# A 272-token encoder layer: the opening laid out by channel, with the squares summed on TensorE and the sine arguments folded on GpSimd

## What is computed

```
h = concatenate([meta, x])                       # 272 x 2048
n = h * rsqrt(mean(h * h, axis=-1) + 1e-6) * norm_g
columns = n @ w_in                               # 2048 x 16384, cut into blocks
z = [t, cos(f w), -sin(f w)]                     # 272 x 33
s = sin(freq * (z @ w1 + b1))
s = sin(freq * (s @ w2 + b2))
s = sin(freq * (s @ w3 + b3))                    # 272 x 64
filters = (s @ w4) * exp(-t * |decay|)
y_a = hyena(u, x1, x2, filters) * silu(gate)     # branch A: long convolution
y_b = fourier(fn_in) * silu(gate)                # branch B: 2-D Fourier transform
y_c = neighbourhood_attention(q, k, v) * silu(gate)
m = g_a * (y_a @ w_a) + g_b * (y_b @ w_b) + g_c * (y_c @ w_c)
out = rmsnorm(h + m @ w_out, final_g)[16:]
```

## Time and profile before

| | us |
|---|---|
| median of 3 runs | 1128.18 |
| lowest, highest | 1127.41, 1128.9 |
| profiled execution | 1127.34 |
| its span in the trace | 1125.5 |
| TensorE busy in the span | 1103.2 |
| VectorE, ScalarE, GpSimd busy | 772.3, 567.1, 61.9 |

### The profile page before, as it was taken

The page is one execution under the profiler, slowest core; times in us unless marked ns, Lnnn a source line. Parts: engine busy times, 40 slices in busy tenths (PEclk is TensorE's granted clock), DMA queues, the critical chain, the costliest instruction groups (busy, mean ns, idle before and its releaser), DMA issues.

```text
span 1125.5 us, 17228 instructions
## 1 busy us (share of the span) xinstructions
PE 1103.2 (98%) x7158; PEld 1005.7 (89%) x7158; DVE 772.3 (69%) x1151; ACT 567.1 (50%) x787; POOL 61.9 (5%) x98
## 2 busy tenths in 40 slices
PE   4999999999999999999999999999999999999997
PEld 2999999999999999999999988888888888888885
DVE  6778888778787688886888785554555455454654
ACT  6655555556545456555554564443444444444443
POOL 4030000300001200002000000000000000000000
PEclk9999999999999999999999999999999999999999
DMA  8744443644335534435543475555555555556652
GB/s 315 241 135 169 150 151 122 205 169 150 135 128 197 186 116 147 151 125 185 188 150 117 160 269 195 202 188 198 187 187 187 192 197 189 201 194 255 231 189 110
DMA packets 30494, 201.54 MB, mean 179 GB/s; under 512 B 3873, under 2 KB 4193, under 8 KB 7745
## 3 DMA queue, kind: packets, MB, share of 16 engines
q1 hardware_dynamic: 25024, 180.16, 45.4%
q0 software_dynamic: 5248, 19.77, 5.3%
q10 hardware_dynamic: 144, 0.52, 0.1%
HBM read 195.19 MB, written 5.24 MB: 178 GB/s over the span
## 4 chain that ended last, share of the span: by engine, by line
PE 98%; DVE 1%; ACT 0%; DMA 0%; issue 0%; DVEq 0%; ACTq 0%
PE ps L574 30%; PE ps L575 30%; PE ps L576 30%; PE ps L579 2%; PE ps L598 1%; PE ps L687 1%; PE ps L727 1%; PE ps L617 1%; PE ps L618 0%; PE ps L718 0%; PE ps L719 0%; PE ps L930 0%; PE ps L729 0%; DMA net<-net_in 0%; PE ps L735 0%; PE ps L737 0%
## 5 line engine op out<-in xcount | busy, mean ns | idle before, releaser
L1328 DVE TENSOR_TENSOR w_lo<-raw,w_hi 128x1024 fp32r<-128x1024 f32 x336 | 409.0, 1230 | 257.8 <-ACT w_hi L988 257.3
L988 ACT ACTIVATE w_hi<-raw 128x1024 fp32r<-128x1024 f32 x336 | 351.2, 1056 | 342.3 <-PE ps L576 340.1
L574 PE MATMUL ps<-xn_hi,w_hi 128*128 128x272 f32 (+2 forms) x1280 | 367.5, 287 | 0.0
L575 PE MATMUL ps<-xn_lo,w_hi 128*128 128x272 f32 (+2 forms) x1280 | 365.7, 286 | 0.0
L576 PE MATMUL ps<-xn_hi,w_lo 128*128 128x272 f32 (+2 forms) x1280 | 365.5, 286 | 0.0
L574 PEld LDWEIGHTS ps<-xn_hi,w_hi 128*128 128x128 f32 x1280 | 242.2, 189 | 2.0
L575 PEld LDWEIGHTS ps<-xn_lo,w_hi 128*128 128x128 f32 x1280 | 241.8, 189 | 0.7
L576 PEld LDWEIGHTS ps<-xn_hi,w_lo 128*128 128x128 f32 x1280 | 242.1, 189 | 0.0
L574 PE MATMUL ps<-w_hi,xg_hi 128*128 128x512 f32 x352 | 137.4, 390 | 0.0
L576 PE MATMUL ps<-w_hi,xg_lo 128*128 128x512 f32 x352 | 137.2, 390 | 0.0
L575 PE MATMUL ps<-w_lo,xg_hi 128*128 128x512 f32 x352 | 137.1, 390 | 0.0
(11 more groups left out here) (265 smaller groups left out, 1394.6 us busy)
## 6 DMA issues: line engine op xcount, KB each, us to landing
raw<-w_stream SPq DMA_DIRECT2D x168, 1024.0 KB, 4.9
branch_y<-ystage POOLq DMA_DIRECT2D x12, 256.0 KB, 3.9
y_raw<-branch_y POOLq DMA_DIRECT2D x3, 1024.0 KB, 7.0
xin<-x SPq DMA_DIRECT2D x2, 1024.0 KB, 6.4
w4s<-w POOLq DMA_DIRECT2D x16, 128.0 KB, 6.0
absd<-decay POOLq DMA_DIRECT2D x8, 256.0 KB, 6.2
h<-x POOLq DMA_DIRECT2D x2, 1024.0 KB, 8.2
rows_t<-rpb POOLq DMA_DIRECT2D x8, 219.0 KB, 6.2
```

The source lines that it names most:

```text
L574: mm(out_ap, a_hi, b_hi, start=first, stop=False)
L575: mm(out_ap, a_hi, b_lo, start=False, stop=False)
L988: A(w_hi[:, w % 2, part, :], raw[:, w % 4, 1024 * part:1024 * part + 1024], ACT.Copy).then_inc(hi_done, 1)
L1328: return V.tensor_tensor(dst, src, hi.bitcast(F32), ALU.subtract)
```

## The change

- **Layout.** The host gives the tokens, meta tokens included, turned: `x_t` has 128 partitions of channels, and on each 16 blocks of 272 tokens. Four transfers (`PIECES`: 5, 5, 4 and 2 blocks) bring them to `x_in`. The 48 transposes go. SyncE starts the first four weight slabs right behind the pieces, without waiting.
- **Sum of squares.** ScalarE squares a piece (`square`), VectorE adds its blocks (`squares_added`, a TENSOR_REDUCE over the block axis, three pieces; the last piece's two blocks are not added), and TensorE adds over the 128 partitions by five float32 products with a matrix of ones, which leaves each token's sum on every partition. ScalarE takes one square root and VectorE one reciprocal of 128x272.
- **Rows.** For each channel block VectorE multiplies by `norm_g` and the reciprocal (`normal`), ScalarE copies the high part (`normal_high`), and VectorE subtracts (`normal_low`). `first_slabs` runs slabs 0 and 1 block by block, both halves for each block.
- **Small network.** ScalarE multiplies the sum by `freq` and adds `freq * b` (`mlp_input`), GpSimd folds in eight dependent steps (`mlp_layer`), of which the second and third layer stand between the issues of its tables. ScalarE takes the sine.
- **Order of the first slabs.** `make_h4`, the filter steps and the weight halves of slabs 2 to 5 are written out in a new order, and the first half of slab 4 runs ahead of `filter_xy(0)`.

```diff
@@ SyncE @@
-            sp.dma_start(xin[0:NM, 2, :], meta).then_inc(x_landed[2], 16)
-            sp.dma_start(xin[:, 0, :], x[0:128, :]).then_inc(x_landed[0], 16)
-            sp.dma_start(xin[:, 1, :], x[128:256, :]).then_inc(x_landed[1], 16)
-            sp.dma_start(ident[:, :], ident_in).then_inc(ident_landed, 16)
-            sp.wait_ge(x_landed[1], 16)
+            for j, (k0, n) in enumerate(PIECES):
+                sp.dma_start(x_in[:, k0:k0 + n, :].rearrange("p k t -> p (k t)"),
+                             x_t[:, L * k0:L * (k0 + n)]).then_inc(x_landed[j], 16)
             for w in range(4):
                 sp.dma_start(raw[:, w, :], w_stream[w]).then_inc(w_landed[w], 16)
+            sp.dma_start(ident[:, :], ident_in).then_inc(ident_landed, 16)
@@ GpSimd @@
+            def pool_linked(ins, n):
+                ins.then_inc(pool_link, 1)
+                pool.wait_ge(pool_link, n)
+
+            def mlp_layer(layer):
+                G = nc.gpsimd
+                n = 7 * layer
+                pool.wait_ge(mlp_in, layer + 1)
+                pool_linked(G.tensor_scalar(red[:, 1, :], red[:, 0, :], 1.0 / TWO_PI, MAGIC, ALU.mult, ALU.add), n + 1)
...
+                for i, part in enumerate((c1, c2, c3)):
+                    pool_linked(G.tensor_scalar(red[:, 2, :], red[:, 1, :], -MAGIC, -part, ALU.add, ALU.mult), n + 2 + 2 * i)
+                    pool_linked(G.tensor_tensor(red[:, 0, :], red[:, 0, :], red[:, 2, :], ALU.add), n + 3 + 2 * i)
+                G.tensor_scalar(red[:, 0, :], red[:, 0, :], CLAMP, -CLAMP, ALU.min, ALU.max).then_inc(mlp_red, 1)
+
+            mlp_layer(0)
+            pool.wait_ge(x_landed[3], 16)
             load_filter(0)
...
@@ TensorE @@
+            def sum_of_squares():
+                pe.wait_ge(ones_set, 1)
+                for j in range(2):
+                    pe.wait_ge(x_part, j + 1)
+                    mm(ps[:, 4, 0:L], ones[:, :], xpart[:, j, :], start=j == 0, stop=False)
+                pe.wait_ge(x_sq, 4)
+                for k in range(2):
+                    mm(ps[:, 4, 0:L], ones[:, :], xsq[:, 5 + k, :], start=False, stop=False)
+                pe.wait_ge(x_part, 3)
+                mm(ps[:, 4, 0:L], ones[:, :], xpart[:, 2, :], start=False, stop=True).then_inc(ss_mm, 1)
+
+            def first_slabs():
+                for k in range(KT):
+                    w, kk = k // 8, k % 8
+                    cols = slice(128 * kk, 128 * kk + 128)
+                    pe.wait_ge(xt_lo, k + 1)
+                    for nt in range(2):
+                        if kk == 0:
+                            pe.wait_ge(lo_done, 2 * w + nt + 1)
+                        last = three(ps[:, nt, 0:L], w_hi[:, w, nt, cols], w_lo[:, w, nt, cols], xn_hi[:, k, :], xn_lo[:, k, :],
+                                     k == 0, k == KT - 1)
...
+                    if k in (0, 8):
+                        mlp_matmul(1 + k // 8)
...
             mlp_matmul(0)
...
+            sum_of_squares()
+            first_slabs()
+            proj_half(2, 2, 0, NM, 0)
             pe.wait_ge(hid_done, 1)
             make_h4(0, 0)
             make_h4(0, 1)
-            proj_slab(1, 0, 1, 0)
+            proj_half(2, 2, 0, NM, 1)
+            proj_half(3, 2, 1, NM, 0)
             make_h4(0, 2)
-            proj_slab(2, 2, 0, NM)
-            proj_slab(3, 2, 1, NM)
+            proj_half(3, 2, 1, NM, 1)
...
@@ VectorE @@
+            def squares_added(j):
+                dve.wait_ge(x_sq, j + 1)
+                at_row, n = 5 * (j % 2), PIECES[j][1]
+                V.tensor_reduce(xpart[:, j, :], xsq[:, at_row:at_row + n, :].rearrange("p k t -> p t k"),
+                                mybir.AxisListType.X, ALU.add).then_inc(x_part, 1)
+
+            def normal(k):
+                V.scalar_tensor_tensor(xsq[:, k % 4, :], x_in[:, k, :], params[:, NGC + k:NGC + k + 1], xrstd[:, :],
+                                       ALU.mult, ALU.mult).then_inc(x_scaled, 1)
+
+            def normal_low(k):
+                dve.wait_ge(xt_hi, k + 1)
+                lo_part(xn_lo[:, k, :], xsq[:, k % 4, :], xn_hi[:, k, :]).then_inc(xt_lo, 1)
```

More of the change, by code:

```diff
@@ L296, in build @@
     at[0] = xin_at
-    xin = place("xin", [128, 3, D])
+    x_in = place("x_in", [128, KT, L])
+    xsq = place("xsq", [128, 10, L])
+    xpart = place("xpart", [128, 3, L])
+    xstd = place("xstd", [128, L])
+    xrstd = place("xrstd", [128, L])
     at[0] = attn_at
@@ L302, in build @@
     hid = place("hid", [HID, L])
+    ones = place("ones", [128, 128])
     assert at[0] <= attn_end
@@ L652, in filter_f, with proj_half @@
                 last.then_inc(kf_mm, 1)
+            def proj_half(w, bank, half, p0, nt):
+                pe.wait_ge(lo_done, 2 * w + nt + 1)
+                for k in range(8):
+                    cols = slice(128 * k, 128 * k + 128)
+                    last = three(ps[:, bank + nt, 0:L - p0], w_hi[:, w % 2, nt, cols], w_lo[:, w % 4, nt, cols],
+                                 xn_hi[:, 8 * half + k, p0:L], xn_lo[:, 8 * half + k, p0:L], half == 0 and k == 0,
+                                 half == 1 and k == 7)
+                last.then_inc(half_used, 1)
@@ L655, in proj_slab @@
             def proj_slab(w, bank, half, p0):
                 for nt in range(2):
-                    pe.wait_ge(lo_done, 2 * w + nt + 1)
-                    for k in range(8):
-                        cols = slice(128 * k, 128 * k + 128)
-                        last = three(ps[:, bank + nt, 0:L - p0], w_hi[:, w % 2, nt, cols], w_lo[:, w % 4, nt, cols],
-                                     xn_hi[:, 8 * half + k, p0:L], xn_lo[:, 8 * half + k, p0:L], half == 0 and k == 0,
-                                     half == 1 and k == 7)
@@ L663, in proj_slab @@
-                    last.then_inc(half_used, 1)
-            def first_slab():
-                for nt in range(2):
-                    pe.wait_ge(lo_done, nt + 1)
-                    for k in range(8):
-                        if nt == 0:
-                            pe.wait_ge(xt_lo, k + 1)
-                        elif k == 4:
-                            turn_x(range(12, KT))
-                        cols = slice(128 * k, 128 * k + 128)
-                        last = three(ps[:, nt, 0:L], w_hi[:, 0, nt, cols], w_lo[:, 0, nt, cols], xn_hi[:, k, :], xn_lo[:, k, :],
-                                     k == 0, False)
-                    last.then_inc(half_used, 1)
-                    if nt == 0:
-                        turn_x(range(8, 12))
+                    proj_half(w, bank, half, p0, nt)
@@ L1224, in channels_high @@
                     ins.then_inc(n1_hi, 1)
[L1226 to L1237 removed]
+            act.wait_ge(xt_lo, KT)
+            envelope(0, 0)
+            envelope(0, 1)
+            split_both(3)
+            evac(-1, "fin", 7)
+            sd_high(0, 0)
+            split(4, 0)
+            sd_high(0, 1)
+            envelope(0, 2)
+            split(4, 1)
+            sd_high(0, 2)
+            split_both(5)
+            act.wait_ge(zeroed, 5)
+            channels_high(0, False)
+            evac(-1, "fgate", 9)
             for c in range(0, CH):
```

230 lines of the change are left out of this document (99 added, 131 removed).

## The result

The changed kernel takes 1132.47 us (median of 5 runs, 1130.57 to 1133.12), the kernel before 1128.18. The ratio is 1.0035, with a 95% interval of 1.0025 to 1.0046: **slower by 4.3 us**. The forecast was 1129.7, slower by 1.5.

A forecast was written before the change was run, and what follows sets the result against it. TensorE, busy 1103.2 of 1125.5 us, bounds the kernel. Opening and blocks gain 4.5 us, turns cost 5.9, the sine chain sets the mark: 63.2 - 61.77 = +1.5; 1127.34 + 1.5 + 0.84 = 1129.7 us; range 1123.3 to 1133.3.

The forecast's parts named there:

- The forecast case: Whole kernel: GpSimd's folding takes turns with VectorE in the blocks; +1.5 us, 1129.7 us; chance 0.37.
- the mark: End of the first filter's products, with slab 4's first half ahead; 61.77 us before, 63.2 predicted.
- rival (b): VectorE's sums before the reciprocal: reading across blocks at half rate, 2.9 us later; +4.4, 1132.6; 0.18 with slow reciprocal.
- Landing, squares: Opening: token pieces land at 6.1, 7.9, 9.3, 9.9 us; ScalarE's squares take 1.3, 1.3, 1.1, 0.7.
- (c): Opening: slab transfers share the engines with token pieces, the last landing at about 15 us; +5, 1134.7; chance 0.05.
- (d): GpSimd's first computing step: previously hidden start-up appears; up to 6 us hidden, all 11.7 costs some 1.5; chance 0.07.
- Sums of squares: VectorE in the opening: 1.6 us for five blocks, 1.3 for four, at 1.1 ns a column; square root at 15.2.
- The blocks, free of turns: Sixteen blocks on VectorE: 10.4 us of steps, 4.5 of weight halves, 1.3 of waits; 16.2 us, ready at 36.9.
- The turns: Blocks: sixteen GpSimd folding steps each hold VectorE 0.45 us, 7.2 in all, 5.9 after absorbed waits.
- TensorE's level: Blocks: if TensorE drops to 1.2 GHz spacing, the mark moves about 1 us more; not in the sum.
- Behind the blocks: From end of slabs 0 and 1 (43.6) to the mark: filter, half slabs, sine chain; 1.8 us of waits included.
- Rival (a): GpSimd's folding beside VectorE's blocks: the engines are little in each other's way; mark -4.2 us, 1124.0; chance 0.33.

The follow-up runs named there:

- e11: Changed kernel with reductions reading neighbouring columns instead of columns 1088 bytes apart (wrong squares, measurement only): +2.2 us over the kernel before, ratio 1.0018.
- e2: Changed kernel with GpSimd doing only the last of its eight folding steps for the second and third layer: -0.2 us against the kernel before, ratio 0.9996.
- e5: Changed kernel with three unread TensorE products behind each of blocks 4 to 13, no extra ones products: +3.2 us over the kernel before, ratio 1.0027.
- e3: Changed kernel with ten unread ones products behind the total and three unread products behind each of blocks 4 to 13: +3.5 us over the kernel before.
- e1: Changed kernel with VectorE adding squares in side-by-side steps instead of reductions across blocks: +4.1 us over the kernel before, ratio 1.0037.
- e6: e4 with the first sine and the second layer's sum and folding ahead of the square root: -0.6 us against the kernel before, ratio 0.9995.
- e4: Changed kernel with the folding of all three layers on VectorE, six steps each: +4.9 us over the kernel before, ratio 1.0041.
- e7: e6 plus side-by-side adds, extra TensorE products, six row buffers and VectorE two rows ahead: -2.4 us against the kernel before, ratio 0.9979.
- e8: e7 plus small unread TensorE products (14, 6 and 3) ahead of the ones products: +0.3 us over the kernel before, ratio 1.0006.
- e9: e7 plus small unread TensorE products placed where TensorE waits anyway (eleven, four and two): -3.5 us against the kernel before, ratio 0.9967.
- e10: Changed kernel with the early order of e6, but all folding still on GpSimd: +2.0 us over the kernel before, ratio 1.0017.

## Why the prediction was right, and where it was not

The forecast case was the right one: slower by a little, with the folding's turns as what decides. The size was short: +1.5 against +5.8 at the mark, +4.3 in the medians. The measured 1132.47 lies above the forecast's own 1127 to 1132 and inside the recorded range, 0.8 us from its upper end. It nearly equals rival (b)'s 1132.6, but that is chance: (b) gave 2.9 us more to the sums, and they made the square root at most 1.8 late. By its own steps:

- **Bound.** Right. TensorE's waits, and its level, moved the time, and from the mark on the two kernels run alike: the first store of branch data is issued at 77.96 before and 83.79 after, again 5.83 apart.
- **Landing, squares.** Right within some tenths: the pieces landed at 6.5, 8.6, 9.8 and 10.5 (6.1, 7.9, 9.3 and 9.9 predicted), the squares took 1.34, 1.34, 1.11 and 0.66 (1.3, 1.3, 1.1, 0.7 predicted). Rivals (c) and (d) did not come: GpSimd's first folding step began at 5.26, behind ScalarE's input, with no delay.
- **Sums of squares.** Mis-sized: 2.48, 2.48 and 1.98 us instead of 1.6, 1.6 and 1.3. This is rival (b), at 1.8 ns a column, between the 1.1 taken and the doubling. e11 shows that the stride alone does it. The row the prediction leaned on, a copy that reads its columns backwards, has neighbouring columns, and said nothing on columns 1088 bytes apart. The square root started at 16.50, 1.8 late. By e11, where it starts at 15.28, 1.2 of that is the stride. The other 0.6 is not; the later landing accounts for most of it, as the first sum began at 7.93 instead of 7.4.
- **Reciprocal.** 1.85 us against 2.0, 6.3 ns a column. The Trainium skill's page VectorE: DVE Perf Modes speaks of a repeat count of 8 in its walkthrough of the pipeline; the estimate of 2.3 us read from it is above the measured 1.85, and the measurement decides.
- **First products.** 19.6 predicted, 21.43 measured; the second half 20.7 and 22.57. Both are the 1.8 of the square root.
- **The blocks, free of turns.** Mis-sized. e2 has them nearly free of GpSimd: from the second half (22.85) to the last low part (41.98) 19.1 us, where the sum had 16.2. The waits for ScalarE were 2.7 us and not 1.3 (0.30, 0.51, 0.33, 0.69, 0.51, 0.33), and a block's two steps took 0.76 and not 0.72. These two make 2.0 of the 2.9.
- **The turns.** Right in kind, too dear in size: 5.9 was predicted, and e2 is 3.4 us shorter over the same stretch. By the rows VectorE loses 0.47 on the first weight half, 0.15 on each of two normalizing steps, 0.57 on each of two low parts and 0.20 on the second weight half, 2.1 a layer; the eight steps of GpSimd so hold it for 0.26 each and not for the 0.45 of the sum. This error and the one above nearly cancel: 22.1 us were predicted for the blocks, and 22.55 measured. The sum was right here by luck.
- **TensorE's level.** The last paragraph of the prediction named it and gave it "about 1 us", and the sum had nothing for it. At the mark it cost 2.1 to 2.4 (e5, e3), more than the sums, though by the medians 1.1 and 0.8, near that "about 1 us". The mistake was to look only at the blocks, where VectorE sets the pace and the first slow stretch cost at most 0.5 us (e5). The price is paid behind them: at 44.59 work for 24 products was ready or about to be, which take 3.0 us in e3 by its spacings, and it took 5.45.
- **Behind the blocks.** Predicted 19.6 from the end of slabs 0 and 1, with 1.8 of waits in it. Measured 20.1, of which 1.1 belongs to the level, and no wait. The predicted pieces without waits give 17.1, and the same pieces took 19.0 in e1, e2, e3 and e6: a half slab 2.82 instead of 2.73, the four products of `fnet_channels` 1.29 instead of 0.7, the filter 2.0 instead of 1.1. Two errors cancelled once more.

Together, at the mark: 1.8 for the opening (1.2 of it the sums' stride), 0.5 for the blocks, 1.6 for TensorE behind the last low part and 0.5 behind slab 1 make the 4.4 between 63.2 and 67.59.

Rival (a) would have given 1124.0; e2 shows that with nearly no turns this order only reaches the kernel before. Its mistake is that of the blocks and the sums.

The prediction had stated the rule on the two engines as one of steps that take turns. The Trainium skill, page SBUF — State Buffer, section "Who interferes with whom", says more exactly that a VectorE instruction with two SBUF inputs contends with a GpSimd instruction that reads SBUF, and that a reduction never does on this chip. The traces agree with both: 1.00 against 0.43 us for the one, 2.48 in any company for the other. With it a large part of what e1 failed to gain could have been foreseen.

**Open.** When TensorE's level falls is not settled. By the clock records of the traces it was at 0.50 in the changed kernel from 43.2 us, with two blocks still to come, to 50.0; in e4 and e11 it lay much the same, from 41.7 to 48.5 and from 39.0 to 45.9; in e1, e7, e8, e9 and e10 wholly within the blocks; in e2 and e6 it did not fall after the first stretch, although TensorE waited there too (1.49 and 1.29 us in e2; 0.85, 0.88, 1.30 and 1.30 in e6). The timed runs of the changed kernel differ in the same way: one took 1130.57 us with a mean granted clock of 0.997, the slowest 1133.12 with 0.991; but another with 0.991 took 1132.41 and one with 0.995 1132.56, so the level is not all of it. And e3 to e11 price the level only together with extra products or another order.

## What to carry to other kernels

Work moved to GpSimd cost nothing beside VectorE's reductions, which read one tile from SBUF (e10); beside steps with two SBUF operands it came back nearly in full (e4). Where a chain makes TensorE wait, look at what is ready behind the chain's end: that queue is what a fall to the 1.2 GHz level makes longer, and products that nobody reads, put into waits and not ahead of ready work, kept the level up in e3, though in e7 to e9 it still fell once. And an instruction whose price is taken from another row needs a row with the same stride, not only the same number of columns.

## What the hardware showed that I had not expected

- A reduction over columns 1088 bytes apart takes 2.48 us for 1360 columns, over neighbours 1.57 (e11).
- Reductions and GpSimd's steps do not hold each other; adds and subtractions of two SBUF tiles do. GpSimd's step goes from 0.41 to 1.27 us, an add of 544 columns from 0.73 to 1.28, one of 272 from 0.44 to 0.88.
- TensorE's level costs other engines time through small products: 64x272 took 1.17 us at 1.2 GHz against 0.67, and in e1 ScalarE and VectorE stood waiting 1.3 us longer for it.
- The granted clock can read 1.00 where the spacing is that of 1.2 GHz. In e6 it does so over 22 to 30 us, where products follow each other by 0.23 us until 28.2, as at 0.50 in the changed kernel. The reason is that the trace of e6 holds no record of the clock before 28.49 us, and the views count a stretch without a record as 1.00. The first record of the kernel before is at 27.05, that of e7 at 14.93, that of e9 at 8.46: so the ones product near 10 us that took 1.25 us in e7 ran where nothing was recorded, and the one that took 0.72 in e9, behind extra work, at a recorded 1.00. Ahead of the first record only the spacing tells the level.
